# A two-block hybrid kernel on one core: how the first block's modulation sums are turned into columns, and how the gate's low-rank product is split

## The chip, the core and the metric

The kernel runs on one core of one Trainium2 chip. The metric is the time of one execution on the device in microseconds. In the profile PE is TensorE (PEld its weight loads), DVE is VectorE, ACT is ScalarE, POOL is GpSimd, SP is the engine that mostly issues DMAs.

## The reference, cut to what matters

Two blocks follow each other. The first is a stack of two hybrid layers (1024 tokens, width 1024). Each is modulated by a vector that is made from a condition; the second block's vectors are made by the same stage. Only what the change touches is shown.

```python
c_act = silu(c)
for l in range(2):
    mod = c_act @ w_mod[l] + b_mod[l]            # 1024 -> 3072
    shift, scale, gate = split(mod, 3)
    h = rms_norm(x, pre_gain) * (1 + scale) + shift
    proj = h @ w_in                              # the last 16 columns are ga
    gate_logits = ga @ gla_gate_w + gla_gate_b   # 16 -> 128
    log_a = log_sigmoid(gate_logits) / 16        # decay of the gated linear attention
    ...                                          # window attention, retention, gated linear attention
    x = x + gate * rms_norm(y @ w_out, post_gain)
```

## The kernel before, in words

Everything is held with features on the partitions and tokens along the free axis. Large products are made in three parts with an operand split in two (`hi` and `lo`): hi by hi, hi by the activations' remainder, and the weights' remainder by hi.

`load_and_modulate` is the opening stage. SP loads the first 16 chunks of the modulation's weights. VectorE works out the arguments of four rope tables (`argument`, four times), ScalarE takes their sines, SP writes these to memory, and the stage ends when they are written. Meanwhile TensorE multiplies the chunks in four groups of four.

`first_block` is written out with no loops on the chip: 4 units (two layers, two halves of 512 tokens; `it` is 0 to 3), each of 32 steps `s`. A step is one weight chunk, 24 products. Beside each step stand pieces of the mixers, at places `at` = 2s and 2s+1 of a table. Every engine has its own program, in program order, and engines meet at semaphores. Nothing is scheduled automatically, so each engine's order is that of the code.

The rest of the modulation (32 groups of 4 chunks, eight to a unit) is threaded through the steps. `mod_step` is TensorE's part. At s%4 = 0 and 1 it makes the products of four chunks into the PSUM bank `bankM`: four partial sums of each output in the four 32-partition strips, where row v of a strip is vector v (there are `VEC` = 3 vectors), and a chunk's 128 outputs along the free axis. At s%4 = 1 ScalarE's `mod_rows` copies the bank to `mod_row`. At s%4 = 2 TensorE multiplies each 128x128 piece of it, as stationary operand, with the constant `vector_rows` (128x3), which adds the four strips and turns outputs onto partitions. VectorE's `mod_columns` then adds the bias, into `mods`. TensorE's next group (s%4 = 0) waits for that sum.

Around the end of a unit, at the next unit's s = 0, VectorE runs `update(it - 1)`: 16 instructions that add the finished unit's output to x, once ScalarE has made the norm (`rstd`).

`gate_rank` is the 16-column product `ga`, 24 instructions into `bankE`, three for each of 8 blocks of the features. ScalarE copies it out and TensorE multiplies it with `gate_w` (line 1405, the first product after that of s = 2).

Of the kernel before, what the change touches and what calls it, by code (L numbers as in the profile page):

```python
# [8 lines left out]
F32 = mybir.dt.float32  # L9
# [4 lines left out]
ALU = mybir.AluOpType  # L14
# [101 lines left out]
def constants():  # L116
# [6 lines left out]
    c["vector_rows"] = (np.arange(P)[:, None] % 32 == np.arange(VEC)[None, :]).astype(f)  # L123
# [66 lines left out]

def load_and_modulate(nc, t, a, sem):

    groups = MOD_FIRST // MOD_GROUP
    with ExitStack() as ctx:
# [19 lines left out]
        @block.sync  # L214
        def _(sp):
            sp.dma_start(cvec[:], a["c"]).then_inc(vec_in, 16)
            sp.dma_start(t["vector_rows"][:], a["vector_rows"]).then_inc(vec_in, 16)
# [12 lines left out]
            sp.wait_ge(t["rope_saved"], 16 * 4 * NB)  # L230

        @block.scalar
        def _(act):
# [11 lines left out]
            for g in range(groups):  # L245
                act.wait_ge(summed, MOD_GROUP * (g + 1))
                if g >= 2:
                    act.wait_ge(turned, g - 1)
                nc.scalar.activation(row[:, g % 2, :], psR[g % 2][:], ACT.Copy).then_inc(row_ready, 1)
            act.wait_ge(small_in, 16 * 3)  # L250
            nc.scalar.activation(t["ga_hi"][:], ga_raw[:], ACT.Copy).then_inc(ga_high, 1)
# [6 lines left out]
        @block.tensor  # L258
        def _(pe):
            def to_columns(g):  # L260
                pe.wait_ge(row_ready, g + 1)
                for c in range(MOD_GROUP):
                    at = VEC * (g * MOD_GROUP + c)
                    last = nc.tensor.matmul(psM[:, at:at + VEC], row[:, g % 2, c * P:(c + 1) * P], t["vector_rows"][:],
                                            start=True, stop=True)
                last.then_inc(turned, 1)
# [12 lines left out]
        @block.vector  # L279
        def _(dve):  # L280
# [15 lines left out]

            nc.vector.memset(t["cact"][:], 0.0).then_inc(cact_ready, 1)
# [7 lines left out]
            link(nc.vector.tensor_tensor(t["ga_lo"][:], ga_raw[:], t["ga_hi"][:].bitcast(F32), ALU.subtract))  # L305
# [10 lines left out]
            link(nc.vector.tensor_tensor(t["mods"][:, 0:MOD_FIRST, :],  # L316
                                         psM[:, 0:VEC * MOD_FIRST].rearrange("p (n v) -> p n v", v=VEC),
                                         t["mod_bias"][:, 0:MOD_FIRST].rearrange("p (n o) -> p n o", o=1)
                                         .to_broadcast([P, MOD_FIRST, VEC]), ALU.add))
# [30 lines left out]
def first_block(nc, t, a, sem):  # L350

    with ExitStack() as ctx:
# [13 lines left out]
        ga = sb("ga", [GATE_RANK, W])  # L366
# [227 lines left out]
        def _(act):  # L594
# [102 lines left out]
            def mixers(it, at):  # L697

                if at == LOGIT_AT - 1:
                    act.wait_ge(*ga_done.after(it, 1))  # L700
                    nc.scalar.activation(ga[:], bankE[0:GATE_RANK, :], ACT.Copy).then_inc(*ga_ready.one)
# [81 lines left out]
            def mod_rows(it, s):  # L783

                g = group_of(it, s)
                act.wait_ge(*mod_summed.after(g, MOD_GROUP))
                if g:
                    act.wait_ge(*mod_turned.after(g - 1, 1))
                nc.scalar.activation(mod_row[:], bankM[:], ACT.Copy).then_inc(*mod_row_ready.one)

# [7 lines left out]
            for it in range(UNITS):  # L798
                for s in range(OUT1):
                    if s % 4 == 1:  # L800
                        mod_rows(it, s)
# [18 lines left out]
                for k in range(KB):  # L820
                    s = OUT1 + k
                    if s % 4 == 1:
                        mod_rows(it, s)
# [20 lines left out]
        def _(dve):  # L844
# [189 lines left out]

            def mod_columns(it, s):
# [4 lines left out]
                nc.vector.tensor_tensor(mods[:, q:q + MOD_GROUP, :],  # L1040
                                        bankM[:, 0:VEC * MOD_GROUP].rearrange("p (n v) -> p n v", v=VEC),
                                        t["mod_bias"][:, q:q + MOD_GROUP].rearrange("p (n o) -> p n o", o=1)
                                        .to_broadcast([P, MOD_GROUP, VEC]), ALU.add).then_inc(*mod_out.one)
# [49 lines left out]
            for it in range(UNITS):  # L1093
# [3 lines left out]
                for s in range(OUT1):  # L1097
                    mixers(it, 2 * s)
# [16 lines left out]
                for k in range(KB):  # L1115
                    s = OUT1 + k
                    if s % 4 == 2:
                        mod_columns(it, s)
# [15 lines left out]
        def _(pe):  # L1134
# [63 lines left out]
            def gate_rank(it):  # L1198

                l = it // NB  # L1200
                for k in range(KB):
                    at = slice(k * GATE_RANK, (k + 1) * GATE_RANK)
# [177 lines left out]
            def mod_step(it, s):  # L1380
# [11 lines left out]
                elif s % 4 == 2:  # L1392
                    pe.wait_ge(*mod_row_ready.after(g, 1))
                    for c in range(MOD_GROUP):
                        last = nc.tensor.matmul(bankM[:, VEC * c:VEC * c + VEC], mod_row[:, c * P:(c + 1) * P], t["vector_rows"][:],
                                                start=True, stop=True)
                    last.then_inc(*mod_turned.one)
# [1589 lines left out]
def program(nc, a, out):  # L2987
    with ExitStack() as ctx:
# [17 lines left out]
        with ExitStack() as first:  # L3006
# [6 lines left out]
            t["vector_rows"], t["mask1"] = sb1("vector_rows", [P, VEC]), sb1("mask1", [P, 2, 2 * P], BF16)  # L3013
            t["ga_hi"], t["ga_lo"] = (sb1(n, [P, DEPTH, P], F32R) for n in ("ga_hi", "ga_lo"))
# [72 lines left out]
```

## Time and profile before

| | us |
|---|---|
| median of 3 runs | 4113.09 (4111.51 to 4115.67) |
| span of the profiled execution | 4110.4 |
| PE busy, of the span | 3780.9 (92%) |
| DVE busy | 2083.4 (51%) |
| ACT busy | 1751.6 (43%) |
| POOL busy | 1777.0 (43%) |

The profiled execution is known by its span, from the first to the last instruction; the times of the three runs are those of the device for a whole execution. The opening stage takes the span's first 54 us, the four units lie between 54 and 1250 us (each some 293 us apart), the second block takes the rest.

### The profile page before, as it was taken

To read this page: it belongs to the slowest core of one execution; us is meant where nothing else is said; L and a number is where in the kernel's file an instruction comes from. 1 tells how busy PE (TensorE), PEld (TensorE's weight loads), DVE (VectorE), ACT (ScalarE), POOL (GpSimd) and SP (SyncE) were. 2 spreads that over 40 slices of the span, in tenths; PEclk is the share of its full clock that TensorE was granted. 3 is DMA by queue.
4 is the path that set the end of the run, shared out by engine and by line. 5 is a ranking of instruction groups with operands and counts; after the bars stand their busy time and mean duration, and the time that the engine had idled before them with its cause. 6 is when DMAs were issued, how large, how long until landed. Compare 5 with 4: busy or idle time off the path is not lost.

```text
span 4110.4 us, 61713 instructions
## 1 busy us (share of the span) xinstructions
PE 3780.9 (92%) x22828; PEld 3037.5 (74%) x22828; DVE 2083.4 (51%) x2741; ACT 1751.6 (43%) x2935; POOL 1777.0 (43%) x1288
## 2 busy tenths in 40 slices
PE   4999999999996899877999899999899889999997
PEld 3767867767775677656888897887677668887886
DVE  5445545545445556657324656226657564336224
ACT  3355355354354444545323454235444453334223
POOL 1443434444432422225545785444422244545444
PEclk8999999999998899988999999999999999999999
DMA  6333433433422321112332453332221123233323
GB/s 245 126 118 118 147 113 122 133 129 128 136 103 92 100 80 48 62 47 82 92 96 93 138 169 102 93 96 82 80 80 57 57 67 95 95 92 94 95 92 102
DMA packets 127204, 421.26 MB, mean 102 GB/s; under 512 B 17408, under 2 KB 19088, under 8 KB 126352
## 3 DMA queue, kind: packets, MB, share of 16 engines
q1 hardware_dynamic: 120080, 407.45, 30.7%
q10 hardware_dynamic: 6912, 10.90, 0.8%
q8 instruction: 143, 2.34, 0.2%
q14 instruction: 69, 0.57, 0.0%
HBM read 397.32 MB, written 6.29 MB: 98 GB/s over the span
## 4 chain that ended last, share of the span: by engine, by line
PE 52%; DVE 8%; ACT 3%; issue 2%; POOL 1%; DMA 0%; SPq 0%; ACTq 0%; DVEq 0%; POOLq 0%
PE lin L2570 28%; PE lin L2579 14%; DVE tmp L2219 2%; PE lin L2828 2%; PE bankO L2699 2%; PE bankT L2637 2%; PE lin L2600 1%; DVE x L2252 1%; DVE y L2251 1%; ACT whi L1850 1%; DVE staged L2231 1%; PE scores L2674 1%; DVE h_lo L2242 1%; PE bankT L2544 1%; POOL wlo L1831 1%
## 5 line engine op out<-in xcount | busy, mean ns | idle before, releaser
L1831 POOL TENSOR_TENSOR wlo<-late_raw,whi 128x512 fp32r<-128x512 f32 x456 | 638.8, 1424 | 817.8 <-PE lin L2579 490.2
L1831 POOL TENSOR_TENSOR wlo<-wraw,whi 128x512 fp32r<-128x512 f32 x452 | 635.2, 1428 | 748.8 <-PE lin L2579 489.9
L2570 PE MATMUL lin<-h_hi,whi 128*128 128x512 f32 (+1 forms) x1856 | 692.1, 380 | 40.2 <-ACT y L2130 14.0
L2570 PE MATMUL lin<-h_lo,whi 128*128 128x512 f32 (+1 forms) x1856 | 679.4, 373 | 0.0
L506 POOL TENSOR_TENSOR wlo<-wraw,whi 128x512 fp32r<-128x512 f32 x260 | 361.1, 1409 | 464.2 <-PE lin L1152 304.5
L2570 PE MATMUL lin<-a_hi,whi 128*128 128x512 f32 (+1 forms) x1280 | 475.9, 379 | 18.1 <-ACT tmp L2139 13.8
L2570 PE MATMUL lin<-a_lo,whi 128*128 128x512 f32 (+1 forms) x1280 | 472.2, 376 | 0.0
L1850 ACT ACTIVATE whi<-late_raw 128x1024 fp32r<-128x1024 f32 x228 | 239.2, 1058 | 535.1 <-PE lin L2570 410.6
L1850 ACT ACTIVATE whi<-wraw 128x1024 fp32r<-128x1024 f32 x226 | 237.3, 1058 | 505.3 <-PE lin L2570 419.7
L2570 PEld LDWEIGHTS lin<-h_hi,whi 128*128 128x128 f32 x1856 | 355.9, 192 | 120.9 <-issue 22.5
L2579 PE MATMUL lin<-h_hi,wlo 128*128 128x512 f32 (+1 forms) x1856 | 429.7, 375 | 1.4 <-POOL wlo L1831 1.0
L2570 PEld LDWEIGHTS lin<-h_lo,whi 128*128 128x128 f32 x1856 | 356.0, 192 | 59.6 <-issue 1.6
L2579 PEld LDWEIGHTS lin<-h_hi,wlo 128*128 128x128 f32 x1856 | 327.9, 191 | 64.0 <-issue 4.1
L2455 DVE TENSOR_TENSOR tmp<-tmp 128x512 f32<-128x512 f32 (+1 forms) x160 | 191.8, 1199 | 336.4 <-ACT tmp L2139 329.6
L1144 PE MATMUL lin<-h_hi,whi 128*128 128x512 f32 x800 | 333.0, 416 | 15.3 <-DVE h_lo L865 15.3
L1144 PE MATMUL lin<-h_lo,whi 128*128 128x512 f32 x800 | 320.9, 401 | 0.0
L2570 PEld LDWEIGHTS lin<-a_hi,whi 128*128 128x128 f32 x1280 | 244.3, 191 | 73.9 <-ACT tmp L2139 21.7
L2579 PE MATMUL lin<-a_hi,wlo 128*128 128x512 f32 (+1 forms) x1280 | 296.7, 376 | 2.0 <-POOL wlo L1831 2.0
L2480 DVE TENSOR_TENSOR y<-lin,y 128x512 f32 (+3 forms) x120 | 76.5, 638 | 400.0 <-PE lin L2579 399.8
L2570 PEld LDWEIGHTS lin<-a_lo,whi 128*128 128x128 f32 x1280 | 244.5, 191 | 46.6 <-issue 0.4
L2579 PEld LDWEIGHTS lin<-a_hi,wlo 128*128 128x128 f32 x1280 | 226.5, 190 | 51.1 <-POOL wlo L1831 3.2
L603 ACT ACTIVATE whi<-wraw 128x1024 fp32r<-128x1024 f32 x130 | 136.7, 1057 | 294.9 <-PE lin L1144 201.6
(364 smaller groups left out, 6591.0 us busy)
## 6 DMA issues: line engine op xcount, KB each, us to landing
wraw<-in_w SPq DMA_DIRECT2D x332, 512.0 KB, 3.6
late_raw<-in_w SPq DMA_DIRECT2D x212, 512.0 KB, 3.5
mod_ring<-in_w_ada SPq DMA_DIRECT2D x96, 512.0 KB, 4.5
mod_ring<-in_w_mod SPq DMA_DIRECT2D x32, 512.0 KB, 4.8
turn<-turn SPq DMA_DIRECT2D x144, 64.0 KB, 2.0
first_ring<-in_w_mod SPq DMA_DIRECT2D x16, 512.0 KB, 17.0
wraw<-in_dft_tokens SPq DMA_DIRECT2D x16, 512.0 KB, 3.9
late_raw<-in_dft_tokens SPq DMA_DIRECT2D x16, 512.0 KB, 3.7
```

Source lines behind the costliest of these rows:

```text
L506: last = nc.gpsimd.tensor_tensor(wlo[:, s, half], wraw[:, s, half], whi[:, s, half].bitcast(F32), ALU.subtract)
L603: nc.scalar.activation(whi[:, s, :], wraw[:, s, :], ACT.Copy).then_inc(*w_hi.one)
L1144: last = nc.tensor.matmul(bank[c % 2], whi[:, c % 2, k * P:(k + 1) * P], h[:, k, :], start=(k == 0 and h is h_hi), stop=False)
L1831: last = nc.gpsimd.tensor_tensor(wlo[:, s, half], raw_chunk[r][:, half], whi[:, s, half].bitcast(F32), ALU.subtract)
L1850: nc.scalar.activation(whi[:, s, 0:D], raw_chunk[r], ACT.Copy).then_inc(*w_hi.one)
L2219: nc.vector.tensor_tensor(total, total, slot[:, 0:w], ALU.add).then_inc(*sig["add"].one)
L2455: nc.vector.tensor_tensor(tmp[:, 2 + s, 0:w], tmp[:, 4 + s, 0:w], tmp[:, 4 + s, 0:w], ALU.mult).then_inc(*a_sq.one)
L2570: last = nc.tensor.matmul(bank[s][:, 0:p.w], whi[:, s, k * P:(k + 1) * P], h[:, k, 0:p.w], start=(k == 0 and h is parts[0]), stop=False)
L2579: last = nc.tensor.matmul(bank[s][:, 0:p.w], wlo[:, s, k * P:(k + 1) * P], parts[0][:, k, 0:p.w], start=False, stop=(k == KB - 1))
L2637: last = nc.tensor.transpose(out, probs[i % 2][:, kv, k * P:(k + 1) * P], ident[:])
L2699: last = nc.tensor.matmul(bankO[half, g * P:(g + 1) * P], v, probsT[:, kv, at:at + P], start=(k == 0), stop=(k == n - 1))
L2828: return nc.tensor.matmul(bank[c][:, 0:2 * P].rearrange("p (t n) -> p t n", t=2), x_part[:, k, cols], w[:, 0:2, k * P:(k + 1) * P], start= ...
```

## The change

Three edits, all in the two stages above.

1. The bank's turn. VectorE, no longer ScalarE, takes `bankM` out, with an instruction that turns each 32x32 block while it copies. Then the outputs lie on partitions within a strip, and one product of the constant `fold` (128x128, ones where row and column agree modulo 32) with 48 columns adds the four strips, for four chunks at once. The sums of a chunk's four quarters lie side by side, so the bias is added by four instructions of 32 partitions each (`biased`) where it was one of 128.
2. In the opening stage the same turn stands on VectorE's queue behind each of the four `argument` calls. ScalarE no longer has the copies, and `fold` (64 KB) is loaded in the place of `vector_rows` (1.5 KB), ahead of the weights.
3. `ga_hi` and `ga_lo` become one operand of 32 columns, `ga_both`. `gate_rank` makes two products for each block of the features (h_hi, h_lo) and no longer three, into 32 rows, and `gate_w` is doubled to 32 rows.

```diff
+def fold_products(nc, out, fold, turned):
+    blocks = turned.rearrange("p (b r) -> p b r", r=32)[:, :, 0:VEC]
+    return nc.tensor.matmul(out.rearrange("p (b v) -> p b v", v=VEC), fold, blocks, start=True, stop=True)
+
+def biased(nc, mods, sums, bias, n):
+    for q in range(4):
+        part = slice(32 * q, 32 * q + 32)
+        last = nc.vector.tensor_tensor(mods[part], sums[part].rearrange("p (n q v) -> p n q v", q=4, v=VEC)[:, :, q, :],
+                                       bias[part].rearrange("p (n o) -> p n o", o=1).to_broadcast([32, n, VEC]), ALU.add)
+    return last
...
             for j in range(2):
                 for cosine in (1, 0):
                     argument(j, cosine)
+                    turn_products(2 * j + 1 - cosine)
...
-            def mod_rows(it, s):
...
-                nc.scalar.activation(mod_row[:], bankM[:], ACT.Copy).then_inc(*mod_row_ready.one)
...
+            def mod_rows(it, s):
+                g = group_of(it, s)
+                dve.wait_ge(*mod_summed.after(g, MOD_GROUP))
+                if g:
+                    dve.wait_ge(*mod_turned.after(g - 1, 1))
+                nc.vector.transpose(mod_row[:], bankM[:]).then_inc(*mod_row_ready.one)
...
                 for s in range(OUT1):
+                    if s % 4 == 1:
+                        mod_rows(it, s)
                     mixers(it, 2 * s)
...
-                    for n, (w, h) in enumerate(((t["ga_hi"], h_hi), (t["ga_hi"], h_lo), (t["ga_lo"], h_hi))):
-                        last = nc.tensor.matmul(bankE[0:GATE_RANK, :], w[:, l, at], h[:, k, :],
-                                                start=(k == 0 and n == 0), stop=(k == KB - 1 and n == 2))
+                    for n, h in enumerate((h_hi, h_lo)):
+                        last = nc.tensor.matmul(bankE[0:2 * GATE_RANK, :], t["ga_both"][:, KB * l + k, :], h[:, k, :],
+                                                start=(k == n == 0), stop=(k == KB - 1 and n == 1))
...
                 elif s % 4 == 2:
                     pe.wait_ge(*mod_row_ready.after(g, 1))
-                    for c in range(MOD_GROUP):
-                        last = nc.tensor.matmul(bankM[:, VEC * c:VEC * c + VEC], mod_row[:, c * P:(c + 1) * P], t["vector_rows"][:],
-                                                start=True, stop=True)
-                    last.then_inc(*mod_turned.one)
+                    fold_products(nc, bankM[:, 0:4 * VEC * MOD_GROUP], t["fold"][:], mod_row[:]).then_inc(*mod_turned.one)
```

VectorE's queue at the start of unit 1. First before: the end of `update` (`gate_y`, `x`), then the bias of group 8.

```order
L884 TENSOR_TENSOR gate_y<-gate_y,rstd 128x512
L885 SCALAR_TENSOR_TENSOR x<-gate_y,cols,x 128x512
L884 TENSOR_TENSOR gate_y<-gate_y,rstd 128x512
L885 SCALAR_TENSOR_TENSOR x<-gate_y,cols,x 128x512
L1040 TENSOR_TENSOR mods<-bankM,mod_bias 128x12
```

Then the same place after the change.

```order
L886 TENSOR_TENSOR gate_y<-gate_y,rstd 128x512
L887 SCALAR_TENSOR_TENSOR x<-gate_y,cols,x 128x512
L886 TENSOR_TENSOR gate_y<-gate_y,rstd 128x512
L887 SCALAR_TENSOR_TENSOR x<-gate_y,cols,x 128x512
L1043 STREAM_TRANSPOSE mod_row<-bankM 128x512
L201 TENSOR_TENSOR mods<-bankM,mod_bias 32x12 x4
```

The bank's turn stands behind all 16 instructions of `update`.

ScalarE's queue before, in unit 0, shows where the copy stood: between the evacuation of step 0 (`gq`) and the split of a weight chunk (`whi`).

```order
L745 ACTIVATE gq<-lin 128x512
L789 ACTIVATE mod_row<-bankM 128x512
L603 ACTIVATE whi<-wraw 128x1024
L701 ACTIVATE ga<-bankE 16x512
L747 ACTIVATE gk<-lin 128x512
```

That row is gone from all 32 places of the units after the change, and its other rows keep their order.

VectorE's queue at s = 24 and 25 of a unit (`turn` are sums of squares for the next unit's norm, `fin` for this one's), before:

```order
L1032 TENSOR_TENSOR h_lo<-aq,h_hi 128x512 x4
L850 TENSOR_TENSOR turn<-turn 128x512
L1123 TENSOR_TENSOR fin<-fin 128x512
L850 TENSOR_TENSOR turn<-turn 128x512 x2
L1040 TENSOR_TENSOR mods<-bankM,mod_bias 128x12
```

and after:

```order
L1034 TENSOR_TENSOR h_lo<-aq,h_hi 128x512 x4
L852 TENSOR_TENSOR turn<-turn 128x512
L1043 STREAM_TRANSPOSE mod_row<-bankM 128x512
L1135 TENSOR_TENSOR fin<-fin 128x512
L852 TENSOR_TENSOR turn<-turn 128x512 x2
L201 TENSOR_TENSOR mods<-bankM,mod_bias 32x12 x4
```

The turn of the unit's seventh group stands between the first sum for the next unit and the first sum for this one.

## Rows read from the trace of the kernel before

**Rows 1.** The page: chain that ended last, share of the span by engine

```profile
PE 52%; DVE 8%; ACT 3%; issue 2%; POOL 1%; DMA 0%; SPq 0%; ACTq 0%; DVEq 0%; POOLq 0%
```

**Rows 2.** `bankM`, unit 0 to 3: engine, operation, count, ns min/median/max, first and last start

```profile
L1395 PE MATMUL bankM<-vector_rows,mod_row x256: 168/252/273, 92.6 to 1234.2; 128*128 128x3 f32 x128
L789 ACT ACTIVATE mod_row<-bankM x32: 590/597/598, 81.7 to 1227.1; 128x512 f32<-128x512 f32 x32
...
  PE bankM L1395: 14.7, 1
```

**Rows 3.** Timeline of PE at an ordinary turn: start us, us, instruction, count, idle before

```profile
205.93 0.95 PE L1395 MATMUL bankM<-vector_rows,mod_row 128*128 128x3 f32 x8
206.74 0.48 PE L1144 MATMUL lin<-h_hi,whi 128*128 128x512 f32 x1
```

**Rows 4.** Timeline of PE from the start of unit 1

```profile
374.37 1.02 PE L1216 MATMUL quad<-fin,ones 128*128 128x512 f32 x2
...
378.19 0.41 PE L1204 MATMUL bankE<-h_hi,ga_hi 128*16 128x512 f32 x1
...
383.54 0.40 PE L1204 MATMUL bankE<-h_hi,ga_lo 128*16 128x512 f32 x1
383.78 0.40 PE L1144 MATMUL lin<-h_hi,whi 128*128 128x512 f32 x1
...
389.26 0.95 PE L1395 MATMUL bankM<-vector_rows,mod_row 128*128 128x3 f32 x8
390.14 1.12 PE L1405 MATMUL quad<-ga,gate_w 16*128 16x512 f32 x2
```

**Rows 5.** Timeline of DVE there: first and last of the 16 instructions of `update`

```profile
379.59 0.90 DVE L884 TENSOR_TENSOR gate_y<-gate_y,rstd 128x512 f32<-128x512 f32 x1 [5.46 <-ACT rstd L621]
...
390.25 1.64 DVE L885 SCALAR_TENSOR_TENSOR x<-gate_y,cols,x 128x512 f32<-128x512 f32 x1
391.92 0.17 DVE L1040 TENSOR_TENSOR mods<-bankM,mod_bias 128x12 f32<-128x12 f32 x1
```

**Rows 6.** Groups of DVE's instructions by line and shape: count, busy us, mean ns

```profile
L993 DVE COPY big<-quad 128x512 f32<-128x512 f32 x32 | 21.9, 684 | 10.2 <-PE quad L1352 9.7
L850 DVE TENSOR_TENSOR turn<-turn 128x512 f32<-128x512 f32 x35 | 37.6, 1074 | 38.1 <-ACT turn L609 36.6 <-DVE turn L850 0.5
```

**Rows 7.** Timeline of DVE: two short instructions with no wait between them

```profile
248.72 0.16 DVE L978 TENSOR_TENSOR sink_arg<-nmax,cols 128x4 f32<-128x4 f32 x1
248.79 0.17 DVE L1040 TENSOR_TENSOR mods<-bankM,mod_bias 128x12 f32<-128x12 f32 x1
```

**Rows 8.** Timelines of PE and DVE at s = 25 and 26 of unit 0

```profile
324.83 0.39 PE L1178 MATMUL lin<-h_hi,wlo 128*128 128x512 f32 x1
325.92 1.05 PE L1395 MATMUL bankM<-vector_rows,mod_row 128*128 128x3 f32 x8 [0.70 <-ACT mod_row L789]
326.83 0.48 PE L1144 MATMUL lin<-h_hi,whi 128*128 128x512 f32 x1
...
325.41 1.11 DVE L850 TENSOR_TENSOR turn<-turn 128x512 f32<-128x512 f32 x1 [8.13 <-ACT turn L609]
```

**Rows 9.** Timelines of DVE and PE at the end of unit 0

```profile
364.65 0.16 DVE L1040 TENSOR_TENSOR mods<-bankM,mod_bias 128x12 f32<-128x12 f32 x1
...
364.87 1.08 PE L186 MATMUL bankM<-mod_ring,cact 128*32 128x128 f32 x32 [0.87 <-DVE mods L1040]
366.48 0.47 PE L1144 MATMUL lin<-h_hi,whi 128*128 128x512 f32 x1 [0.53 <-DVE h_lo L865]
```

**Rows 10.** Timeline of the opening stage

```profile
25.60 0.69 DVE L295 TENSOR_SCALAR arg<-arg 128x1024 f32<-128x1024 f32 x1
26.21 0.69 DVE L288 TENSOR_SCALAR turns<-ang 128x1024 f32<-128x1024 f32 x1
...
27.45 0.60 ACT L249 ACTIVATE first_row<-psR 128x512 f32<-128x512 f32 x1 [3.76 <-PE psR L186]
...
48.99 1.06 ACT L254 ACTIVATE arg<-arg 128x1024 f32<-128x1024 f32 x1 [3.33 <-DVE arg L295]
...
54.22 0.32 SPq L483 DMA_DIRECT2D rope<-rope_tables  x1
```

**Rows 11.** Windows: from:to, us, busy (x) of PE, PEld, DVE, ACT, POOL; clock; DMA share, GB/s

```profile
404.20:408.00 3.80, 1.05 (x33) 0.80 (x33) 0.98 (x1) 3.74 (x7) 1.10 (x2) 0.99 0.00 0
408.01:414.80 6.79, 6.79 (x44) 5.61 (x45) 3.86 (x3) 2.23 (x4) 6.79 (x7) 0.50 0.26 80
...
218.30:221.80 3.50, 0.35 (x2) 0.00 (x0) 1.25 (x2) 3.47 (x11) 0.00 (x0) 1.00 0.41 116
221.90:225.30 3.40, 3.40 (x30) 2.30 (x34) 0.68 (x1) 3.04 (x4) 0.00 (x0) 1.00 0.00 0
...
366.50:370.30 3.80, 1.96 (x6) 0.84 (x6) 3.80 (x4) 0.85 (x2) 2.65 (x2) 1.00 0.14 9
370.40:373.80 3.40, 3.40 (x9) 2.69 (x9) 3.37 (x6) 0.00 (x0) 0.00 (x0) 0.50 0.84 340
```

**Rows 12.** Timelines of ACT and POOL before the first level of unit 1

```profile
402.36 2.01 ACT L603 ACTIVATE whi<-wraw 128x1024 fp32r<-128x1024 f32 x2 [7.09 <-PE lin L1167]
...
406.20 0.63 ACT L655 ACTIVATE big<-big 128x512 f32<-128x512 f32 x1
...
406.90 0.73 POOL L532 TENSOR_TENSOR big<-gk,big 128x256 f32<-128x256 f32 x1 [6.82 <-ACT big L655]
```

More of the change, by code:

```diff
@@ L216, in _ @@
             sp.dma_start(cvec[:], a["c"]).then_inc(vec_in, 16)
-            sp.dma_start(t["vector_rows"][:], a["vector_rows"]).then_inc(vec_in, 16)
+            sp.dma_start(t["fold"][:], a["fold"]).then_inc(vec_in, 16)
             for m in range(MOD_GROUP):
@@ L244, in _ @@
             nc.scalar.activation(t["cact"][:, :, 0:VEC], cvec[:], ACT.Silu).then_inc(cact_ready, 1)
[L245 to L249, printed above, removed]
             act.wait_ge(small_in, 16 * 3)
-            nc.scalar.activation(t["ga_hi"][:], ga_raw[:], ACT.Copy).then_inc(ga_high, 1)
+            nc.scalar.activation(t["ga_both"][:, :, 0:GATE_RANK], ga_raw[:].rearrange("p l (k n) -> p (l k) n", n=GATE_RANK),
+                                 ACT.Copy).then_inc(ga_high, 1)
             for n in range(4):
@@ L261, in to_columns @@
                 pe.wait_ge(row_ready, g + 1)
-                for c in range(MOD_GROUP):
-                    at = VEC * (g * MOD_GROUP + c)
-                    last = nc.tensor.matmul(psM[:, at:at + VEC], row[:, g % 2, c * P:(c + 1) * P], t["vector_rows"][:],
-                                            start=True, stop=True)
-                last.then_inc(turned, 1)
+                at = 4 * VEC * MOD_GROUP
+                fold_products(nc, psM[:, at * g:at * (g + 1)], t["fold"][:], row[:, g % 2, :]).then_inc(turned, 1)
             pe.wait_ge(cact_ready, 2)
@@ L295, in argument, with turn_products @@
                 nc.vector.tensor_scalar(out, out, -PI_IN, None, ALU.max).then_inc(args_ready, 1)
+            def turn_products(g):
+                dve.wait_ge(summed, MOD_GROUP * (g + 1))
+                if g >= 2:
+                    dve.wait_ge(turned, g - 1)
+                nc.vector.transpose(row[:, g % 2, :], psR[g % 2][:]).then_inc(row_ready, 1)
             nc.vector.memset(t["cact"][:], 0.0).then_inc(cact_ready, 1)
@@ L315, in _ @@
             dve.wait_ge(turned, groups)
[L316 to L319, printed above, removed]
+            link(biased(nc, t["mods"][:, 0:MOD_FIRST, :], psM[:, 0:4 * VEC * MOD_FIRST], t["mod_bias"][:, 0:MOD_FIRST], MOD_FIRST))
             pre_columns(nc, t, link, 0)
@@ L365, in first_block @@
         gate_y = sb("gate_y", [P, KB, W])
-        ga = sb("ga", [GATE_RANK, W])
+        ga = sb("ga", [2 * GATE_RANK, W])
         big, fin, turn = sb("big", [P, KB, W]), sb("fin", [P, 4, W]), sb("turn", [P, 4, W])
@@ L700, in mixers @@
                     act.wait_ge(*ga_done.after(it, 1))
-                    nc.scalar.activation(ga[:], bankE[0:GATE_RANK, :], ACT.Copy).then_inc(*ga_ready.one)
+                    nc.scalar.activation(ga[:], bankE[0:2 * GATE_RANK, :], ACT.Copy).then_inc(*ga_ready.one)
                 if at == LOGIT_AT:
@@ L1039, in mod_columns @@
                 dve.wait_ge(*mod_turned.after(g, 1))
[L1040 to L1043, printed above, removed]
+                biased(nc, mods[:, q:q + MOD_GROUP, :], bankM[:, 0:4 * VEC * MOD_GROUP], t["mod_bias"][:, q:q + MOD_GROUP],
+                       MOD_GROUP).then_inc(*mod_out.one)
                 dve.wait_ge(*mod_out.after(g, 1))
@@ L1116, in _ @@
                     s = OUT1 + k
+                    if s % 4 == 1:
+                        mod_rows(it, s)
                     if s % 4 == 2:
@@ L3012, in program @@
             t["mod_ring"], t["cact"] = sb1("mod_ring", [P, MOD_RING, D]), sb1("cact", [P, KB, 32])
-            t["vector_rows"], t["mask1"] = sb1("vector_rows", [P, VEC]), sb1("mask1", [P, 2, 2 * P], BF16)
-            t["ga_hi"], t["ga_lo"] = (sb1(n, [P, DEPTH, P], F32R) for n in ("ga_hi", "ga_lo"))
+            t["fold"], t["mask1"] = sb1("fold", [P, P]), sb1("mask1", [P, 2, 2 * P], BF16)
+            t["ga_both"] = sb1("ga_both", [P, DEPTH * KB, 2 * GATE_RANK], F32R)
             for name in CONSTS1[2:]:
@@ L3054 @@
     a["sinks1"] = np.broadcast_to(inp["attn_sinks"], (P, DEPTH, 8))
-    a["gate_w"] = inp["gla_gate_w"].transpose(1, 0, 2)
+    a["gate_w"] = np.tile(inp["gla_gate_w"].transpose(1, 0, 2), (2, 1, 1))
     a["w1"] = np.stack([np.concatenate([chunked(inp["w_in"][l][:, order1]), chunked(inp["w_out"][l][out_rows])])
```

16 lines of the change are left out of this document (3 added, 13 removed).

## Prediction

> **What bounds the kernel now.** I began with the page. Its chain of work that ended last lies on TensorE for 52% and on VectorE for 8% [rows 1], so what counts is what TensorE has to issue and what it waits for. Then I took the instructions on the bank of the modulation, to see what one turn costs and who waits [rows 2]: 256 records of products (two passes to each of four products, 32 times) and 32 copies of 0.597 us on ScalarE. The timelines around single turns follow. An ordinary turn holds TensorE from 205.93 to 206.74, 0.81 us, with dense products on both sides [rows 3]. So whatever is taken off a turn there comes off the path, unless a wait takes its place. Whether one does depends on where VectorE stands when TensorE arrives. I therefore compared for all 32 groups the end of the last VectorE instruction that will stand ahead of the turn with TensorE's arrival. In 25 of them VectorE is free microseconds before. The other seven are the unit starts of units 1 to 3 and s = 26 of every unit, and the rows for one of each stand ahead [rows 4, 5, 8].
>
> **The change part by part.**
>
> *The turn on TensorE.* Eight records in 0.81 us are 0.10 us each [rows 3]. Two remain (two passes of one product). I take 6 x 0.10 = 0.60 us off. The new ones have 48 columns and not 3, read with a stride. No row shows such a product: at 0.23 us for 512 columns [rows 4] 48 columns are 0.02 us and stay hidden under the weight load. If they were not hidden the saving would be some 0.50 us, and it cannot be above the whole 0.81. This saving reaches the path in 21 groups: the first of unit 0, and s = 6, 10, 14, 18 and 22 of every unit. **21 x 0.60 = -12.6 us.**
>
> *The gate's products.* The 24 products run from 378.19 to 383.78, 0.233 us each [rows 4]. Eight fewer are 1.86 us a unit. Thirty-two stationary columns instead of 16 don't show where the moving side has 512. In unit 0 nothing waits behind them, since VectorE is idle for 14.7 us until that turn [rows 2]. **-1.9 us, once.** In units 1 to 3 they only bring TensorE sooner to the next wait.
>
> *The turn on VectorE.* It reads 128x512 from PSUM and writes it to SBUF, as the copy that takes 684 ns [rows 6]. No row shows a block transpose. I take 0.69 us, with 1.07 us as the upper end (the mean of a sum of that size while GpSimd works too, rows 6 as well); less than 0.6 has no row behind it. The Trainium skill, VectorE: DVE Perf Modes, section on the three transpose paths, gives 311 ns for VectorE's 128x128 in bf16; four of those, as an estimate from that page, would be 1.24 us, and the sum below would be 5.5 us higher.
>
> *Unit starts, units 1 to 3.* VectorE's queue now reads `update`, then the turn. `update` begins when ScalarE has the norm, 379.59, and its last instruction ends at 391.89 [rows 5]. TensorE stood at the turn at 389.26 and will be there 1.86 us sooner, at 387.40 [rows 4]. The block turn takes from 391.9 to 392.6, so TensorE starts at 392.65, after a wait of 5.25 us. Against before that is 3.39 later, less the 0.60: +2.79 us, and the gate's saving is swallowed. The product queued behind is that of `gate_w` [rows 4], and the whole of the decay's work on ScalarE, VectorE and GpSimd waits for it. **3 x 2.79 = +8.4 us.** VectorE's start of `update` hangs on TensorE's own sum (374.37) through ScalarE, so it doesn't come sooner.
>
> *The clock after that wait.* Before, TensorE's granted clock is 0.50, the 1.2 GHz level, from 408.01 to 414.80, after 3.8 us in which it was busy for 1.05; the same shows in 3.4 us after a stretch of short waits (366.50 to 370.30). After the 3.50 us from 218.30, with 0.35 busy, it stays at 1.00 [rows 11]. The new wait is longer than all of these, with dense products around it. The bounds are nothing (as at 221.90) and 3.4 us a time (6.8 us at half clock). The nearest is the 3.4 us at half clock, 1.7 us of loss; a part of it may pass within the wait. I take 1.3. **3 x 1.3 = +3.9 us.** The Trainium skill, TensorE: Matmul & The Clock Gate, Part 1, says that the throttled clock is the default and that activity releases it. By that rule every such wait costs something; the row at 221.90 shows one that did not.
>
> *s = 26, four times.* TensorE has waited here for ScalarE's copy already and starts at 325.92. VectorE is in a sum from 325.41 to 326.52, which itself waits for ScalarE [rows 8]. Its turn ends at 327.2, TensorE starts at 327.3: 1.35 later, less 0.60. **4 x 0.75 = +3.0 us.**
>
> *Bias in four parts, and s = 30.* Two short instructions without a wait between them start 0.07 us apart [rows 7]; three more are 0.24 us. TensorE reads that result at once only at a unit's end: it waits 0.87 us for it, and next for the `h_lo` behind it on VectorE's queue [rows 9]. **4 x 0.24 = +1.0 us**, and for the same reason the 0.60 saved at s = 30 is lost, because this stretch starts with ScalarE's norm work, ahead of s = 30. If VectorE's sums were not late there, the 0.60 would count too (-2.4 in all).
>
> *The opening stage.* It ends when the last rope table is written, at 54.22, 5.2 us after the last sine began, which waited for VectorE's last argument [rows 10]. Ahead of that argument VectorE now makes three turns. The first can't start before TensorE's group 0 is summed, 27.45, where the next chain started at 26.21. With 0.61 from start to start it goes on at 28.06: +1.85. Two more are +1.22. The 62 KB more ahead of the positions load is put at 0.15. **+3.2 us.** The fourth turn and the four sums come after and lie beside the sine and the writes. ScalarE's early sines add no DMA traffic, they move it. The bounds are 2.0 (part of it hidden) and 4.4 (1.07 us a turn).
>
> *ScalarE.* It is rid of 32 x 0.597 us [rows 2]. Where TensorE waits for ScalarE the copies do not stand ahead, except at s = 26, which is counted. I count nothing.
>
> *Sum:* -12.6 - 1.9 + 8.4 + 3.9 + 3.0 + 1.0 + 3.2 = **+5.0 us**. It is made against the profiled execution's span, 4110.4, which lies 2.7 below the median of 4113.1. The difference carries over: **4118 us**.
>
> **The rivals.** What a measurement can tell from no change is about 0.2%, 8.2 us here: 4104.9 to 4121.3.
>
> *A, the forecast:* waits at the three unit starts, each with a short drop of the clock, 4114 to 4121. Chance 0.45.
>
> *B, the clock holds.* As after 218.30 [rows 11]. Then it is 1.1 above before, **4114.2**. Against it: the wait is 5.25 us and not 3.5. Chance 0.18.
>
> *C, slower: the clock stays down.* If each wait is followed by 6.8 us at 0.50, as at 408.01, that is 3 x 3.4 and the sum is +11.3, **4124.4**. It decides from 2.4 us a wait on. For it: that stretch follows a shorter wait than the new one. Against it: there the products before and behind the wait are small ones, 32 wide and 64 columns; here they are dense. A turn on VectorE that takes 1.07 us adds 0.38 at ten places (three in the opening stage, three unit starts, four at s = 26), +3.8 by itself, 4122. By the page's estimate of 1.24 us it would be 4123.6. Chance together 0.22.
>
> *D, the unit starts' wait is taken back.* 15 us after it TensorE waits for GpSimd's first keys already, from before 408.01 [rows 11]. If those hung on something that doesn't move with TensorE, the 2.79 and the drop would vanish in it: 5.0 - 8.4 - 3.9 = -7.3, **4105.8**. But GpSimd waits there for ScalarE, and ScalarE for TensorE's products (7.09 us) [rows 12], so it moves along. Chance 0.10.
>
> *E, the wait isn't there.* If `update` came to its end before TensorE, the unit starts would each give 0.60 + 1.86: -12.6 - 1.9 - 7.4 + 7.2 = -14.7, **4098.4**. `update` would have to end 5.2 us sooner. Chance 0.05.
>
> **How the numbers follow.** The time is that of A. A, B, C and D together reach from 4105.8 to 4124.4. With a turn on TensorE that saves 0.50 for 0.60 (+2.1) and the rest of the kernel (the second block is untouched, but its short waits move against the clock), I set the range at 4106 to 4125; it leaves out E and half of what lies above C. A alone is 4114 to 4121. Slower is C and the upper edge of A: 0.25. Faster is E and half of D: 0.10. The rest is the same: 0.65.
>
> **What would show it.** At the start of units 1 to 3 TensorE should be idle for about 5 us before the one product of the turn, released by VectorE's turn, and `update` should end just ahead of it; afterwards products of 512 columns either 0.43 apart (clock down) or 0.23. Ordinary turns should take 0.2 to 0.3 us. At s = 26 TensorE should wait 2 us for VectorE. The 16 products of the gate should take 3.7 us. The opening stage should end near 57.4. The prediction is wrong in size if the block transpose takes far from 0.69 us, and wrong in kind if units 1 to 3 come out shorter than before: unit 0 should be shorter by some 4.5 us (3.6 of turns and 1.9 of the gate, less 1.0), the others longer by some 2 (2.8 and 1.3 and 1.0, less 3.0).

## The result and the profile after

The changed kernel is slower: median 4131.7 us (7 runs) against 4117.1 of the kernel before beside it, ratio 1.0035, 95% interval 1.0026 to 1.0045, so 11 to 19 us more. The profiled execution of it has a span of 4129.2, 18.8 above that of before. 4118 was forecast, within 4106 to 4125. That forecast stood on 4113.1, the median of three runs; against the seven beside the changed kernel it would be 4122, so of the difference itself 5.0 was forecast and 14.6 measured. One run of all those below, 6015 us at a mean granted clock of 0.57 (in the experiment with the filled wait), is left out of its ratio.

The turn itself came out as priced or better. Of the instructions on the bank, here by engine, count, ns min/median/max, first and last start:

```profile
L201 DVE TENSOR_TENSOR mods<-bankM,mod_bias x128: 137/166/177, 93.9 to 1265.9; 32x12 f32<-32x12 f32 x128
...
L194 PE MATMUL bankM<-mod_row,fold x64: 205/275/448, 93.6 to 1252.8; 128*128 128x48 f32 x64
L1043 DVE STREAM_TRANSPOSE mod_row<-bankM x32: 716/717/718, 84.5 to 1247.4; 128x512 f32<-128x512 f32 x32
```

VectorE's block turn of 128x512 takes 0.717 us (0.69 was taken; the estimate of 1.24 from the figure of the Trainium skill, VectorE: DVE Perf Modes, the three transpose paths, does not agree), the four parts of the bias 0.70 us together. On TensorE an ordinary turn, the place of [rows 3]:

```profile
203.98 0.32 PE L194 MATMUL bankM<-mod_row,fold 128*128 128x48 f32 x2
204.12 0.48 PE L1156 MATMUL lin<-h_hi,whi 128*128 128x512 f32 x1
```

0.14 us from start to start and not 0.81: 0.67 saved, 0.60 was taken. The gate is shorter too, as the start of unit 1 shows (timeline of PE; compare [rows 4]):

```profile
377.63 0.41 PE L1215 MATMUL bankE<-h_hi,ga_both 128*32 128x512 f32 x1
...
381.10 0.40 PE L1215 MATMUL bankE<-h_lo,ga_both 128*32 128x512 f32 x1
381.33 0.39 PE L1156 MATMUL lin<-h_hi,whi 128*128 128x512 f32 x1
...
385.65 1.29 PE L1164 MATMUL lin<-h_hi,wlo 128*128 128x512 f32 x5
393.19 0.66 PE L194 MATMUL bankM<-mod_row,fold 128*128 128x48 f32 x2 [6.24 <-DVE mod_row L1043]
393.78 2.07 PE L1413 MATMUL quad<-ga,gate_w 32*128 32x512 f32 x2
...
414.62 1.29 PE L1237 MATMUL quad<-fin,big 32*128 32x64 f32 x17 [2.77 <-POOL big L546]
```

Sixteen products take 3.70 us. Then TensorE waits 6.24 us for VectorE's turn. The first level's product (L1237) starts 36.99 us after the gate; before it was 29.82 (378.19 to 408.01, [rows 4, 11]). So this stretch is 7.2 us longer, and in units 2 and 3 it is 7.0 to 7.1 longer: 21 us in all, more than the whole 18.8. Of the 7.2, 4.5 us lie ahead of the turn's product (15.56 us behind the gate's start where it was 11.07) and 2.7 behind it. VectorE there (compare [rows 5]):

```profile
387.57 1.75 DVE L886 TENSOR_TENSOR gate_y<-gate_y,rstd 128x512 f32<-128x512 f32 x1
389.36 1.63 DVE L887 SCALAR_TENSOR_TENSOR x<-gate_y,cols,x 128x512 f32<-128x512 f32 x1
...
392.42 0.72 DVE L1043 STREAM_TRANSPOSE mod_row<-bankM 128x512 f32<-128x512 f32 x1
```

And the granted clock ahead of the turn, behind it, and at three other places (windows; the column behind POOL's is the clock):

```profile
386.80:393.20 6.40, 0.16 (x2) 0.01 (x1) 6.19 (x7) 0.60 (x1) 3.35 (x2) 0.76 0.28 70
393.20:400.30 7.10, 7.10 (x25) 5.51 (x26) 1.52 (x8) 3.86 (x5) 0.00 (x0) 0.50 0.04 13
...
366.30:373.00 6.70, 5.86 (x13) 4.16 (x14) 6.67 (x10) 0.00 (x0) 1.43 (x1) 0.50 0.57 192
523.40:526.70 3.30, 3.30 (x12) 2.07 (x14) 0.68 (x1) 3.01 (x4) 0.00 (x0) 0.50 0.00 0
414.10:420.80 6.70, 6.18 (x42) 5.22 (x43) 3.67 (x4) 2.75 (x5) 6.70 (x7) 0.50 0.26 81
```

Behind the wait TensorE works 7.1 us at half clock and loses about 3.5. The low stretch at the unit's end is 6.7 us where it was 3.4 [rows 11], and one at 523.4, behind a wait for ScalarE, has none to match it in the kernel before. The one from 414.10, at the wait for GpSimd's keys, the kernel before has too, at 408.01 [rows 11]. What TensorE waited for in all four units (engine waited for, us in total, times, longest):

```profile
PE bankM L194 <- DVE mod_row L1043: 27.1, 7, 6.2
...
PE bankM L186 <- DVE mods L201: 6.2, 3, 2.1
```

The second of these was in the kernel before:

```profile
PE bankM L186 <- DVE mods L1040: 2.6, 3, 0.9
```

Seven waits for VectorE's turn are the seven places that the prediction named. The opening stage is 2.7 us longer: the first instruction behind it on SP's queue, at 54.22 before [rows 10], is here

```profile
56.94 0.32 SPq L497 DMA_DIRECT2D rope<-rope_tables  x1
```

### The profile page after: what moved, and what is told of

It is laid out like the page before. It is cut to its first block, busy times and chain, and to the rows that moved or that the text cites. A ratio compares the mean times of both kernels' runs of the same rounds, so it can differ in the third digit from the quotient of the medians.

```text
span 4129.2 us, 61301 instructions
## 1 busy us (share of the span) xinstructions
PE 3768.3 (91%) x22580; PEld 3023.2 (73%) x22580; DVE 2126.0 (51%) x2876; ACT 1733.3 (42%) x2899; POOL 1779.4 (43%) x1288
## 4 chain that ended last, share of the span: by engine, by line
PE 52%; DVE 8%; ACT 3%; issue 2%; POOL 1%; DMA 0%; SPq 0%; ACTq 0%; DVEq 0%; POOLq 0%
PE lin L2578 28%; PE lin L2587 14%; DVE tmp L2227 2%; PE lin L2836 2%; PE bankO L2707 2%; PE bankT L2645 1%; PE lin L2608 1%; DVE x L2260 1%; DVE y L2259 1%; DVE staged L2239 1%; ACT whi L1858 1%; PE scores L2682 1%; PE bankT L2552 1%; DVE h_lo L2250 1%; POOL wlo L1839 1%
```

## The experiments

Two theories. **1:** the loss is made at the starts of units 1 to 3, where VectorE's turn stands behind `update`; TensorE waits there and then works at half clock. **2:** VectorE's added work, the block turn or the opening stage cost wherever they stand. All kernels below were timed in turns with the kernel before, whose median was 4114.4 to 4117.3; ratios are to it. The traces are of one execution each.

**The turn ahead of `update`.** The changed kernel with

```diff
                 if it:
+                    mod_rows(it, 1)
                     update(it - 1)
                 for s in range(OUT1):
-                    if s % 4 == 1:
+                    if s % 4 == 1 and not (it and s == 1):
                         mod_rows(it, s)
```

> The changed kernel with one thing moved: in units 1 to 3 VectorE's turn of the first group stands ahead of the 16 instructions of update and not behind them. Theory 1 (the loss is made at the three unit starts, by TensorE's wait for that turn and by the low clock behind it): each start, which cost 6.9 us more than before, now costs 2.5 us less than before, so 28 us come off the changed kernel: about 4104 us, some 13 below the kernel before. TensorE does not wait at the turn, and the clock is at 1.00 behind it. Theory 2 (VectorE's added work costs wherever it stands, and the opening stage costs the rest): no more than 3 us a start come back, 4122 us or more.

Measured: 4102.1 us, ratio 0.9958 (0.9946 to 0.9970). VectorE's and TensorE's timelines at the start of unit 1:

```profile
375.31 0.72 DVE L1043 STREAM_TRANSPOSE mod_row<-bankM 128x512 f32<-128x512 f32 x1 [4.07 <-PE bankM L186]
376.58 0.89 DVE L886 TENSOR_TENSOR gate_y<-gate_y,rstd 128x512 f32<-128x512 f32 x1 [0.55 <-ACT rstd L635]
...
375.17 0.42 PE L1216 MATMUL bankE<-h_hi,ga_both 128*32 128x512 f32 x1
...
382.56 1.98 PE L1165 MATMUL lin<-h_hi,wlo 128*128 128x512 f32 x8
384.38 0.32 PE L194 MATMUL bankM<-mod_row,fold 128*128 128x48 f32 x2
...
402.51 0.96 PE L1238 MATMUL quad<-fin,big 32*128 32x64 f32 x25 [2.76 <-POOL big L546]
```

The turn fits into time in which VectorE would wait for the norm, and TensorE doesn't wait. The place of one instruction, three times, is worth 30 us: the change becomes a gain of 0.4%. Theory 1's number was 4104. The two traces also split the loss of the late place: from the gate's start to the turn it is 9.21 us and not 15.56, and from the turn to the first level's product 18.13 and not 21.43. So a late turn costs 6.3 us of waiting and 3.3 us of low clock each time.

**The same place for a plain copy.** The kernel before, with only the copy moved from ScalarE to VectorE, at the changed kernel's places:

```diff
-                nc.scalar.activation(mod_row[:], bankM[:], ACT.Copy).then_inc(*mod_row_ready.one)
+                nc.vector.tensor_copy(mod_row[:], bankM[:]).then_inc(*mod_row_ready.one)
```

> The kernel before with one thing changed: the bank is copied out by VectorE, at the places where the changed kernel has its turns, and no longer by ScalarE; four products with vector_rows, the three-part gate and the opening stage as before. Theory 1: TensorE waits 3.4 to 4.5 us at the start of units 1 to 3 and has a low clock behind it (1.5 to 3.5 us each), and 1.35 us at s = 26 four times: 20 to 29 us above the kernel before, 4137 to 4146 us. Theory 2 (the place does not matter, the turned layout or the opening stage does): within 6 us of the kernel before, 4117 to 4123 us.

Measured: 4148.2 us, ratio 1.0078 (1.0065 to 1.0091), 31 us more: above the upper end of theory 1's range, and far outside the other's. At the start of unit 1 TensorE waits for 3.28 us, and the clock is low behind it (behind the same wait in unit 2 the low stretch lasts 3.4 us and not 6.7):

```profile
391.80:395.10 3.30, 0.07 (x1) 0.00 (x0) 3.22 (x4) 0.60 (x1) 3.08 (x2) 1.00 0.00 0
396.80:403.50 6.70, 6.70 (x29) 5.90 (x28) 1.84 (x6) 3.86 (x5) 0.00 (x0) 0.50 0.19 72
```

**The copy on VectorE at early places.** The kernel of the run before, with the copy ahead of `update`, and that of s = 25 ahead of the first sum for the next unit:

```diff
                 if it:
+                    mod_rows(it, 1)
                     update(it - 1)
                 for s in range(OUT1):
-                    if s % 4 == 1:
+                    if s % 4 == 1 and not (it and s == 1):
                         mod_rows(it, s)
...
+                mod_rows(it, OUT1 + 1)
                 for k in range(KB):
                     s = OUT1 + k
-                    if s % 4 == 1:
+                    if s % 4 == 1 and k > 1:
                         mod_rows(it, s)
```

> The kernel before with the copy of the bank on VectorE (four products with vector_rows, three-part gate), but at the early places: ahead of update, and at s = 25 ahead of the first sum for the next unit. Theory 1 (the place makes the loss, not the engine): the 31 us that the same copy cost at the late places are gone, and the 0.9 us a unit that TensorE waited for ScalarE's copy at s = 26 too: 3 to 4 us below the kernel before, about 4113 us. If VectorE's added 22 us of work cost wherever they stand, 4120 us or more.

Measured: 4113.7 us, ratio 0.9997 (0.9988 to 1.0006). The interval holds no change and theory 1's 3 to 4 us less (0.9991). Against the run before it, the same copies on the same engine, only ordered otherwise, are 0.8% apart. So VectorE's load is not the cause.

**The wait filled with products.** The changed kernel, with products that nothing reads ahead of TensorE's wait:

```diff
+                    if it and s == 2:
+                        for _ in range(24):
+                            nc.tensor.matmul(four[2], h_hi[:, 0, 0:P], h_hi[:, 0, :], start=True, stop=True)
                     pe.wait_ge(*mod_row_ready.after(g, 1))
```

> The changed kernel with 24 products more in units 1 to 3 (h_hi by h_hi into a part of quad that nothing reads, 5.5 us) just ahead of TensorE's wait for the turn. They fill most of the 6.2 us wait. Theory 1, its clock part: the clock stays at 1.00 behind the turn and the 3.5 us of half clock at each start go, 4121 us. If the low clock has another cause (the small products behind the wait), the time stays within 2 us of the changed kernel, 4130 to 4134.

Measured: 4109.7 us, ratio 0.9987 (0.9976 to 0.9998): 20 us less than the changed kernel with 72 products more, where 10.6 was expected. Timeline of PE and windows behind the turn:

```profile
383.73 5.60 PE L1406 MATMUL quad<-h_hi 128*128 128x512 f32 x24
390.11 0.42 PE L194 MATMUL bankM<-mod_row,fold 128*128 128x48 f32 x2 [0.79 <-DVE mod_row L1043]
```

```profile
390.10:397.00 6.90, 6.89 (x49) 6.08 (x50) 2.42 (x10) 3.87 (x5) 0.00 (x0) 1.00 0.03 10
397.00:405.00 8.00, 8.00 (x105) 7.61 (x107) 3.54 (x5) 2.31 (x3) 2.07 (x2) 1.00 0.01 2
...
408.30:415.10 6.80, 6.76 (x83) 5.59 (x84) 3.72 (x3) 2.93 (x6) 6.80 (x7) 1.00 0.28 80
```

The turn's product comes as late behind the gate's start as in the changed kernel (15.60 us, and 15.56 there), but the clock stays at 1.00, and from there to the first level's product it is 18.23 us and not 21.43. That is 3.2 us a time, about as expected (3.5). Two more things make up most of the rest, and neither is a part of what the change added. The low stretch behind the first level, which the changed kernel (414.10) and the kernel before (408.01) both have, doesn't come here, which is worth up to 3.4 us a time; how the filling keeps it away is not shown. And unit 0, in which the two kernels are the same, is 2.8 us shorter in this trace (290.4 us from its gate to that of unit 1, and 293.2): so much can two executions of the same code differ.

**The changed kernel with the long gate** (`ga` and `gate_w` with 16 rows again):

```diff
-                    for n, h in enumerate((h_hi, h_lo)):
+                    for n, (w, h) in enumerate(((0, h_hi), (0, h_lo), (1, h_hi))):
```

> The changed kernel with the gate's product in three parts again (24 products of 16 columns for 16 of 32). Theory 1: the gate's saving was swallowed by the wait at the start of units 1 to 3 and reached the end in unit 0 alone, so the time is 1.9 us above the changed kernel, less what a wait shorter by 1.9 us saves in clock (up to 1.7 us each): 4128 to 4134 us. Rival: the saving counted in every unit, then it is 7.4 us above, 4139 us.

Measured: 4125.6 us, ratio 1.0023 (1.0012 to 1.0034). That is below the changed kernel and not above it (the intervals overlap, so I read it as not slower), with 32 products more. TensorE's wait is 3.3 us instead of 6.2. From the gate's start to the first level's product the traces have 34.2 to 35.7 us, where the changed kernel has 36.8 to 37.0, although the gate itself takes 1.9 longer. The rival's 4139 is out.

**The gate alone,** in the kernel before (the operand and `ga` with it as in the change):

```diff
-                    for n, (w, h) in enumerate(((t["ga_hi"], h_hi), (t["ga_hi"], h_lo), (t["ga_lo"], h_hi))):
-                        last = nc.tensor.matmul(bankE[0:GATE_RANK, :], w[:, l, at], h[:, k, :],
-                                                start=(k == 0 and n == 0), stop=(k == KB - 1 and n == 2))
+                    for n, h in enumerate((h_hi, h_lo)):
+                        last = nc.tensor.matmul(bankE[0:2 * GATE_RANK, :], t["ga_both"][:, KB * l + k, :], h[:, k, :],
+                                                start=(k == n == 0), stop=(k == KB - 1 and n == 1))
```

> The kernel before with the gate's product as 16 products of 32 columns and nothing else changed. No turn waits for VectorE then, so the saving counts in every unit: 7.4 us below the kernel before, 4110 us. If the wider operand cost time, or something else waited at the unit starts, less than 3 us come off.

Measured: 4100.0 us, ratio 0.9965 (0.9953 to 0.9976), 14 us less, about double the 7.4 of issue time. A low stretch is shorter: behind TensorE's wait before the first level, where [rows 11] have 6.79 us at 0.50, it has

```profile
400.00:402.50 2.50, 0.62 (x23) 0.65 (x24) 1.57 (x2) 2.46 (x6) 1.73 (x2) 1.00 0.00 0
402.50:406.00 3.50, 3.50 (x27) 2.80 (x23) 2.01 (x2) 0.35 (x1) 3.50 (x5) 0.51 0.21 23
406.00:409.00 3.00, 3.00 (x35) 2.30 (x33) 1.43 (x1) 1.80 (x3) 3.00 (x4) 1.00 0.38 153
```

This low stretch is halved in all three units, and that of 3.4 us at the unit's end (370.40 in [rows 11]) doesn't come at all. From one gate's start to the next, units 1 and 2 take 290.1 us, 3.6 to 3.8 less than before: 1.9 of it are the products, the rest is about what the halved stretch gives back (1.7).

**The gate alone, padded** with eight products more:

```diff
+                    nc.tensor.matmul(four[2][0:2 * GATE_RANK, :], t["ga_both"][:, KB * l + k, :], h_hi[:, k, :], start=True, stop=True)
```

> The kernel before with the gate's 16 products of 32 columns and 8 products more of the same kind whose result nothing reads, so 24 as before. The gate alone came out 16 us below the kernel before where its 32 products less by 0.233 us are 7.4. If the rest of the gain hangs on TensorE's issue time too (the clock's low stretches fall otherwise when the gate is shorter), this is the kernel before again, 4114 to 4119 us. If it is the operand of 32 columns that does it, some 8 us remain, 4108 us.

Measured: 4113.6 us, ratio 0.9997 (0.9987 to 1.0006), the kernel before again. So the whole gain of the gate hangs on the time that TensorE issues, and none on the width of the operand. Its low stretches are again those of the kernel before, at 370 and 408. How the shorter gate makes them shorter is not shown by these two.

**Both late turns moved ahead.** As the first experiment, and at s = 25:

```diff
+                mod_rows(it, OUT1 + 1)
                 for k in range(KB):
                     s = OUT1 + k
-                    if s % 4 == 1:
+                    if s % 4 == 1 and k > 1:
                         mod_rows(it, s)
```

> The changed kernel with two turns moved ahead on VectorE's queue: that of the first group of units 1 to 3 (as in the run that moved it alone, 4102 us), and that of s = 25 in all four units, from behind the first sum for the next unit to ahead of it. Theory 1 (TensorE's wait for VectorE's turn at s = 26 costs, 2.3 us each, and brings low stretches of the clock): the four waits go, 9 us below 4102, about 4093 us, and up to 1.7 us each more where a low stretch goes. If the product behind the turn would have had to wait for something else, no more than 3 us come off (the 0.75 by which the wait grew): 4099.

Measured: 4087.7 us, ratio 0.9934 (0.9921 to 0.9947): the fastest form, 0.66% below the kernel before. At s = 26 TensorE goes on at once (compare [rows 8]):

```profile
321.29 0.40 PE L1192 MATMUL lin<-h_hi,wlo 128*128 128x512 f32 x1
321.53 0.32 PE L194 MATMUL bankM<-mod_row,fold 128*128 128x48 f32 x2
321.67 0.48 PE L1158 MATMUL lin<-h_hi,whi 128*128 128x512 f32 x1
```

Against the turn ahead of `update` alone that is 10 us less by the ratios (0.9958) and 14 by the medians, which come from different sessions. The four waits by themselves were put at 9, so theory 1 holds, and the rival's 3 is too small. In the trace of the first experiment a low stretch of 3.4 us follows two of the four waits of 2.1 us (one from 615.96, 1.1 us behind the turn's last product); here none stands at these places.

**That, with the long gate,** both turns moved ahead as in the last diff and the gate as before the change:

```diff
-                    for n, h in enumerate((h_hi, h_lo)):
+                    for n, (w, h) in enumerate(((0, h_hi), (0, h_lo), (1, h_hi))):
```

> The kernel with two turns moved ahead (4088 us) with the gate in three parts again. What remains against the kernel before is the turn by one product at early places: 32 turns by 0.65 us and 0.9 us at s = 26 four times, less 2.8 us in the opening stage and 0.6 at each unit end: 19 us below the kernel before, about 4098 us. By the rival that the gate makes nearly all of the gain, no more than 8 us below it.

Measured: 4099.2 us, ratio 0.9962 (0.9948 to 0.9976). The turn at early places is worth 16 us (19 were expected), the gate another 12 on top. At late places the same turn and gate together were a loss of 15.

**The opening stage of before** in the changed kernel (its first turns by ScalarE's copy and products with `vector_rows` again):

```diff
+                nc.scalar.activation(row[:, g % 2, :], psR[g % 2][:], ACT.Copy).then_inc(row_ready, 1)
...
-                fold_products(nc, psM[:, at * g:at * (g + 1)], t["fold"][:], row[:, g % 2, :]).then_inc(turned, 1)
...
+                    last = nc.tensor.matmul(psM[:, at:at + VEC], row[:, g % 2, c * P:(c + 1) * P], t["vector_rows"][:],
+                                            start=True, stop=True)
...
-                    turn_products(2 * j + 1 - cosine)
```

> The changed kernel with the opening stage of before alone (both turns at their late places). 2.8 us below the changed kernel, 4129 us; by the theory that the opening stage made most of the loss, 4120 us or less.

Measured: 4125.3 us, ratio 1.0025 (1.0016 to 1.0034). Against the changed kernel's 1.0035 that is 4 us less, with overlapping intervals; 4120 or less is just outside. So it doesn't make most of the loss.

**The opening stage of before, with both turns moved ahead:** the diff above and, in the main loop, both moves as in the experiments above:

```diff
+                    mod_rows(it, 1)
                     update(it - 1)
...
+                mod_rows(it, OUT1 + 1)
```

> As the kernel with the two turns moved ahead, with the opening stage of the kernel before (ScalarE copies, four products with vector_rows, no turns between VectorE's arguments; fold is loaded later). The opening stage of the changed kernel was 2.8 us longer: 2.8 us below the kernel with two turns moved, about 4090 us. If the opening stage's time is made by something else than VectorE's three turns, no difference.

Measured: 4086.1 us, ratio 0.9931 (0.9917 to 0.9944), no difference from 0.9934 that can be told. The traces show 2.1 us (first square on ScalarE at 54.71, here, and 56.85); in the measured times so small a difference can't be seen.

**The unit's end filled,** in the kernel with both turns moved ahead:

```diff
+                    if it and s == 0:
+                        mask = mask1[:, 1, :].rearrange("p (o k) -> p o k", o=1).to_broadcast([P, 2, 2 * P])
+                        for _ in range(10):
+                            nc.tensor.matmul(four[2].rearrange("p (g k) -> p g k", g=2), t["identb"][:], mask, start=True, stop=True)
```

> The kernel with two turns moved ahead (4088 us) and ten products more, whose result nothing reads, at the end of units 0 to 2 ahead of TensorE's wait of 2.2 us for the last bias. Behind that wait the clock is at 0.50 for 6.8 us in this kernel. If it is the wait that brings the clock down here too, the low stretch goes or halves, 1.7 to 3.4 us a unit end: 4078 to 4083 us. If TensorE's later short waits for h_lo bring it down, or products of constants don't count, no change, 4086 to 4089.

Measured: 4090.3 us, ratio 0.9946 (0.9934 to 0.9958), no gain. The low stretch behind the unit's end did halve, but this trace has others, at places that had 1.00 in the trace of the kernel without the filling. First this kernel, then that one:

```profile
363.60:366.90 3.30, 3.11 (x7) 2.44 (x8) 3.30 (x6) 0.00 (x0) 0.00 (x0) 0.50 0.67 218
401.10:404.40 3.30, 3.30 (x9) 2.54 (x8) 1.06 (x1) 0.56 (x1) 3.30 (x4) 0.50 0.31 87
506.90:510.20 3.30, 3.30 (x9) 2.32 (x7) 0.38 (x1) 2.99 (x4) 0.00 (x0) 0.50 0.00 0
```

```profile
362.80:369.50 6.70, 6.30 (x14) 4.48 (x15) 6.54 (x10) 0.00 (x0) 0.95 (x1) 0.50 0.62 190
...
401.00:404.40 3.40, 3.19 (x41) 2.81 (x42) 2.62 (x3) 1.17 (x3) 3.40 (x4) 1.00 0.02 5
506.90:510.20 3.30, 3.30 (x42) 2.29 (x40) 0.06 (x1) 2.94 (x5) 0.00 (x0) 1.00 0.00 0
```

That the filling brought them is not shown. The kernel of the experiment before this one has the same main loop with no filling, and its trace has low stretches at the same two places (29 and 135 us behind the gate's start, as here):

```profile
395.20:398.50 3.30, 3.30 (x9) 2.53 (x8) 0.82 (x1) 0.78 (x2) 3.30 (x4) 0.53 0.36 127
500.90:504.20 3.30, 3.30 (x12) 2.07 (x15) 0.69 (x1) 2.99 (x4) 0.00 (x0) 0.51 0.00 0
```

## Why the prediction was wrong

The mechanism was the right one: the places, the wait and the low clock were named, and moving the turn ahead takes the loss away. The sum was 5.0 where 14.6 was measured (18.8 in the profile). What failed most is the size of one term, **the clock after that wait**: 1.3 us at each unit start was taken between bounds of 0 and 3.4. TensorE worked 7.1 us at half clock behind the wait, and the stretch behind the turn is 3.3 us shorter where the clock stays up (the first experiment; 3.2 in the filled wait). So the term was at its upper bound. I took the rows of 370.40 as the nearest, 3.4 us of half clock, and subtracted from them; those of 408.01, 6.8 us of half clock behind a wait shorter than the new one, were nearer, and they had been set aside as rival C. That rival's sum, +11.3 (4124.4), is the nearest to what came.

This term is 6 us of the 14 that the sum lacks against the profile. The wait itself was 1.1 us longer each time than forecast, 3 us in all. The other 5 us lie in the rest of units 1 to 3, 1.6 us a unit: the waits for the bias grew by 3.6 us over three unit ends where 1.0 was counted in all, and the low stretches at the unit's end and at 523.4, which the sum put at nothing, are longer or new. What each of these two costs was not measured, so for 5 of the 14 us the cause is open in part.

Point by point:

- *The turn on TensorE:* 0.67 us saved, for 0.60. Right, also with the early places: 16 us.
- *The gate:* right that units 1 to 3 swallow it. What was missed: a saving ahead of a wait lengthens the wait, here from 3.3 to 6.2 us. Of these 2.9 us 1.9 are the gate's and 1.1 a longer `update` (see the unit starts below). It made the changed kernel no faster, maybe slower. Where nothing waits it is worth 14 us and not 7.4.
- *The turn on VectorE:* 0.717 for 0.69. Right. The estimate of 1.24 us from the figure of the Trainium skill, VectorE: DVE Perf Modes, was 0.5 us too high.
- *Unit starts:* the wait was 5.25 in the forecast and 6.24 in the trace. `update` is longer by an instruction pair slowed to 1.75 and 1.63 us (before, one was slow, 1.64 us, [rows 5]), while GpSimd works on the next chunk, once TensorE's products let it. That is 8.0 us behind the start of `update` (387.09), where it was 10.0 before (389.57) and is 9.9 with the long gate, and there one instruction is slow. So TensorE's being done sooner moves GpSimd's work onto two of VectorE's instructions.
- *s = 26:* the wait went from 1.1 to 2.5 us from product to product, the next product came 0.75 later, as forecast. Moving it away brought 10 us by the ratios, a little more than the 8.5 us that TensorE waited there in all: a wait of 2.1 us can have its own low stretch behind it, which the sum put at nothing.
- *Bias in four parts:* 0.70 us and not 0.40. The spacing of 0.07 [rows 7] holds for one pair of instructions on the same 128 partitions; these four, each on 32 partitions of its own, stood 0.18 apart. TensorE's waits for the bias went from 2.6 to 6.2 us over three unit ends.
- *The opening stage:* +2.7 us in the trace for 3.2. Right.
- *ScalarE:* nothing, right.
- *Units by themselves:* the gate's start in unit 1 came at 377.63 and before at 378.19, with an opening stage 2.7 longer: unit 0 is 3.3 shorter (4.5 forecast). Units 1 to 3 were to be some 2 longer each and are 6.3 to 6.8 longer.

The low clock's part in the other stretches (the unit ends, 523.4) is seen in the traces. Which wait brings down which of them was tried once, at the unit's end, and stays open, and with one trace a kernel so does how far they vary from one execution to the next.

## What to carry to other kernels

Where an instruction that the bottleneck waits for changes engines, look for the place in the new engine's queue before anything else: on the same engine the same 32 copies cost 31 us or nothing. A wait of 3 to 6 us on a dense TensorE cost its length here and then 1.6 to 3.3 us in clock, so price it by the nearest row of half clock behind a shorter wait, not by a fraction of it. And a saving that TensorE makes just ahead of a wait can come to nothing or, as the traces here have it, to a small loss; the same edit should be timed again once the wait is gone.

## What was not expected of the hardware

- The size of the low stretches: behind waits of 3.3 and 6.2 us TensorE worked 6.7 (in one unit 3.4) and 7.1 us at 1.2 GHz, while 5.6 us of products that nothing reads in the same gap kept it at 2.4 GHz.
- Low stretches come and go with small things. Eight products fewer in the gate halved one of 6.8 us. In unit 0 the changed kernel's trace has 3.3 us at 0.50 from 219.50, and that of the filled wait, with the same code there, has 1.00. Effects of 3 us a unit can come from that alone, either way.
- VectorE's block turn of 128x512 from PSUM took 0.717 us in all 32 places, in 29 of them with GpSimd busy beside it and in three without. The sums of `update` between two SBUF tensors took 0.69 us alone and up to 1.75 with GpSimd busy.
